# Final output blocks stored from two queues instead of three, and cached keys turned and loaded at other places

## The chip, the core and the metric

The kernel runs on one core of a Trainium2 chip. A core has five engines, each with its own instruction stream, which meet only through semaphores: TensorE (PE in the profile) multiplies matrices into PSUM banks, VectorE (DVE) and ScalarE (ACT) do elementwise work, reductions and the way out of PSUM, GpSimd (POOL) makes masks and issues transfers, and SyncE (SP) only issues transfers. A transfer is issued by one instruction of SP, ACT or POOL and carried out by the core's 16 DMA engines. The metric is the time of one execution on the device in microseconds. Lower is better.

## What is computed

A streaming encoder step with two layers, on 16 meta tokens and 256 new frames of one stream and 32 frames of a running one (304 columns in all, width 2048). All matrices are float32.

```python
for layer in range(DEPTH):                    # DEPTH = 2
    if layer < N_A:                           # layer 0: mLSTM, 8 heads of 512, then the shared K/V
        xp, buf, C, n, m = mlstm_layer(xp, ...)
        xs, buf, C, n, m = mlstm_layer(xs, state_conv[i], state_C[i], state_n[i], state_m[i], ...)
        p_k, p_v, p_logf = shared_kv(xp, kv_norm_g, w_kvf, b_f, k_norm_g)
        s_k, s_v, s_logf = shared_kv(xs, kv_norm_g, w_kvf, b_f, k_norm_g)
        ks_all = concatenate([cache_k, s_k], axis=1)     # 512 cached rows + 32 new ones
        vs_all = concatenate([cache_v, s_v], axis=1)
    else:                                     # layer 1: forgetting attention ("FoX"), 16 heads of 128
        xp = fox_layer(xp, qpos_p, fp[:, N_META:], p_k, p_v, ...)
        xs = fox_layer(xs, qpos_s, fs[:, past:], ks_all, vs_all, ...)

def fox_layer(x, ...):
    q, z = split(rmsnorm(x, norm_g) @ w_in, 2)
    q = rmsnorm(q, q_norm_g)
    o = fox_attend(q, f_q, q_pos, k, v, f_k, k_pos)   # softmax(q k^T + forget terms) v
    return x + (o * silu(z)) @ w_out                  # y_prompt (256 rows) and y_sample (32 rows)
```

The change touches the second layer only: the cached keys and values that the running stream attends to, and the stores of y_prompt and y_sample at the very end.

## The kernel before

The columns are the tokens; the residual stream lies in SBUF turned, as xT (128 partitions, 16 parts of the width, 304 columns). Every weight matrix is streamed through four slots in chunks of 512 rows x 256 columns. For each chunk SP loads it into `raw` (L147), ScalarE makes a rounded copy `w_hi` (L153), VectorE the rest `w_lo` = raw - w_hi (L158), and TensorE does three products for each of eight 128x128 pieces (L178 to L180, 24 matmuls). The semaphore `used` counts the chunks that TensorE has finished, `lo_made` the low parts. ScalarE and VectorE work two chunks ahead of TensorE, and SP may load a slot again once its low part is made.

The attention layer is one list, `order`, of 96 chunks that all engines walk through alike. Q chunks give queries of a group of four heads, Z chunks the gates, OUT chunks multiply with w_out. The list is Q0, then Z0 and Q1, then Z1, Q2 and OUT0, then Z2, Q3 and OUT1, then Z3 and OUT2, and OUT3 at the end, eight chunks each. Each chunk is a slot, to which the tables `QUERIES`, `ATTEND` and `BESIDE` attach events of the attention. In slot n each engine does its part of chunk n (VectorE and ScalarE: the low and high part of chunk n+2), then its part of the slot's events, strictly in that order. The events that matter here, for a group g:

- `q`: TensorE turns the queries to token rows, ScalarE takes them (q_t) and squares them. `r`: VectorE sums the squares (L2567) and scales them (L2570). `n`: ScalarE takes the root (L2463). `f`: VectorE finishes the norms and scales q_t (L210 to L218, L2590, L2593). `s`: VectorE copies two selection matrices (L2583, L2584). `b`: TensorE turns the queries back (L2767), VectorE takes them (qT L2604, q_new L2607).
- `K0` to `K3`: VectorE turns the cached keys Kc of one head into KcT (L2577, `turn_keys`). The first of a group waits until all 16 loads of its keys have landed. Each counts up `blk_made`.
- `X0`, `Y`: TensorE computes the first scores (L2779 to L2781, which need q_new and qT), and the scores with the cached keys (L2793, which need all four KcT).

GpSimd issues the group's loads: 16 for the cached keys (`kc_load`, L2395), the gains (L2401), the new keys (L2405) and three for values (`v_load`, L2408 to L2412). For the first group it does so on its way from the step before; for a later one it waits until the four KcT of the group before are made.

During OUT3 the output is finished: after chunk j VectorE adds the product to xT (L2670), turns two parts of the width into `y_blk` (L2677) and counts up `blk_made`. The function `y_store` then stores the block with 12 transfers: four bands of partitions `a`, each with two parts for y_prompt (L2367, 32 KB each) and one for y_sample (L2371, 8 KB). `Y_PARTS` divides them among three engines, four each: share 0 goes to SP, share 1 to ScalarE (one slot late, behind that slot's high part), share 2 to GpSimd. SP starts on them after its last chunk load. At the end SP waits for the stores of its own and ScalarE's, GpSimd for its own.

Of the kernel before, what the change touches and what calls it, by code (L numbers as in the profile page):

```python
# [44 lines left out]
GROUPS = BH // GRP  # L45
# [55 lines left out]
def settled(own, cell):  # L101

    own.wait()
    own.done(own.eng.tensor_tensor(cell, cell, cell, ALU.mult))  # L105

def trunk(nc, i, o):
    whole = ExitStack()
    with whole:  # L110
        def sem(name):
            return whole.enter_context(nc.semaphore(name))
# [24 lines left out]
        used = sem("used")  # L137
# [1623 lines left out]
        C_FOX = C_OUT + 16 * GROUPS  # L1761
# [47 lines left out]
        def fox_load(sp, n, kind, g, j):  # L1809

            if kind == "OUT":
                load_chunk(sp, n, i["b_w_out"][0, HD * g:HD * (g + 1), CW * j:CW * (j + 1)])
            else:
                col = HD * g + CW * (j // 4) + (D if kind == "Z" else 0)
                load_chunk(sp, n, i["b_w_in"][0, 512 * (j % 4):512 * (j % 4 + 1), col:col + CW])
# [22 lines left out]
        def store_values(eng, g, done):  # L1838
            store(eng, g, "v", v_t, done)
            cols_ = bass.ds(g.times(HD).value, HD)  # L1840
            eng.dma_start(v2_dram[0:256, cols_].rearrange("(t p) c -> p t c", p=P), v_t[:, 0:2, :])\
               .then_inc(done, 16)
            eng.dma_start(v2_dram[256:T, cols_], v_t[0:TAIL, 2, :]).then_inc(done, 16)
# [314 lines left out]
        def kv_tensor(pe):  # L2158
# [87 lines left out]
            def last_values():  # L2246
# [53 lines left out]

        ATTEND = {5: "X0 Y", 6: "E0 EY", 7: "N0 NY X1", 8: "T0 TY E1 z", 9: "OY O0 N1 X2", 10: "T1 E2", 11: "O1 N2 X3",
                  12: "T2 E3", 13: "O2 N3", 14: "T3", 15: "O3"}
        QUERIES = {0: "q", 1: "r n K0 K1", 2: "f K2 K3", 3: "s", 4: "b"}

        BESIDE = {0: {**QUERIES, **ATTEND}, 1: {**QUERIES, **ATTEND, 16: "q", 17: "r", 18: "n", 19: "f", 20: "s", 21: "b"},
                  2: {1: "K0 K1", 2: "K2 K3", **ATTEND, 16: "q", 17: "r", 18: "n", 19: "f", 20: "s", 21: "b"},
# [1 line left out]
        BESIDE[3][7], BESIDE[3][8] = "T0 TY E1", "z OY O0 N1 X2"  # L2308
        PARTS_NEXT = {1: "H0 H1", 2: "H2 H3"}
        PARTS_LAST = {9: "H0", 11: "H1", 13: "H2", 15: "H3"}  # L2310
        Y_PARTS = (((0, (0, 1, 2)), (3, (0,))), ((1, (0, 1, 2)), (3, (1,))), ((2, (0, 1, 2)), (3, (2,))))

        order, at = [], A_FOX

# [34 lines left out]
        def use(g, e, k=0):  # L2349
            return USE[g, e] + k  # L2350

        def freed(eng, u):

            eng.wait_ge(use_free[u % 4], u // 4 + 1)
# [4 lines left out]
        def y_store(eng, j, share, stored):  # L2359

            eng.wait_ge(blk_made, BLK_Y + j + 1)
            for a, parts in Y_PARTS[share]:
                rows_ = slice(32 * a, 32 * a + 32)
                for part in parts:
                    if part < 2:
                        c = P * (2 * j + part) + 32 * a
                        eng.dma_start(o["y_prompt"][0, :, c:c + 32].rearrange("(b i) c -> i b c", i=32),  # L2367
                                      y_blk[rows_, 2 * j + part, 0:SEQ].rearrange("i (b c) -> i b c", c=32))\
                           .then_inc(stored, 16)
                    else:  # L2370
                        eng.dma_start(o["y_sample"][0].rearrange("i (k a j) -> a i k j", a=4, j=32)[a][:, 2 * j:2 * j + 2, :],  # L2371
                                      y_blk[rows_, 2 * j:2 * j + 2, SEQ:TQ]).then_inc(stored, 16)

        def fox_sync(sp):
            for n, kind, g, j, _, _ in order[SLOTS:]:
                fox_load(sp, n, kind, g, j)
                if (kind, g, j) == ("Z", 0, 0):
                    for b in range(3):
                        sp.wait_ge(t_free[b], 3 * GROUPS)
                    store_values(sp, Count(GROUPS - 1), last_out)  # L2380
            for j in range(8):
                y_store(sp, j, 0, y_stored)
            sp.wait_ge(y_stored, 16 * 8 * 8)

        def fox_gpsimd(pool):
            own = Own(pool, pool_own, counted["pool"])

            def heads(g):
                return slice(g * HD, (g + 1) * HD)

            def kc_load(g):
                for x in range(GRP):
                    for a in range(4):
                        src = i["cache_k"][0, :, GRP * g + x, 32 * a:32 * a + 32].rearrange("(b j) d -> j b d", j=32)
                        pool.dma_start(Kc[32 * a:32 * a + 32, x, :].rearrange("j (b d) -> j b d", d=32), src)\  # L2395
                            .then_inc(kc_landed, 16)

            def gq_load(g):
                src = i["q_norm_g"][0].rearrange("h d -> (h d)")[heads(g)]
                for m in range(GRP):  # L2400
                    pool.dma_start(gq[:, m:m + 1], src[m * P:(m + 1) * P].rearrange("(p a) -> p a", a=1))\  # L2401
                        .then_inc(gq_landed, 16)

            def kt_load(g):
                pool.dma_start(kT_in[:, :, :], kT_dram[g]).then_inc(kt_landed, 16)  # L2405

            def v_load(g):
                pool.dma_start(Vc[:, :, :], i["cache_v"][0].rearrange("(t p) h d -> p t (h d)", p=P)[:, :, heads(g)])\  # L2408
                    .then_inc(v_landed, 16)
                pool.dma_start(v_all[:, 0:2, :], v2_dram[0:256, heads(g)].rearrange("(t p) c -> p t c", p=P))\  # L2410
                    .then_inc(v_landed, 16)
                pool.dma_start(v_all[0:TAIL, 2, :], v2_dram[256:T, heads(g)]).then_inc(v_landed, 16)  # L2412

            pool.wait_ge(used, C_FOX)
            settled(own, cell[:, :])
            kc_load(0)
            gq_load(0)
            kt_load(0)
            pool.wait_ge(fox_set, 2)  # L2420
            v_load(0)
            pool.wait_ge(last_out, 80)
            for g in range(1, GROUPS):
                pool.wait_ge(blk_made, BLK_KC + GRP * g)
                settled(own, cell[:, :])
                kc_load(g)
                for t in range(3):
                    freed(pool, use(g - 1, "b", t))
                settled(own, cell[:, :])
                gq_load(g)  # L2430
                pool.wait_ge(use_ready, use(g - 1, "X3") + 1)
                settled(own, cell[:, :])
                kt_load(g)
                pool.wait_ge(use_ready, use(g - 1, "O3") + 1)
                settled(own, cell[:, :])
                v_load(g)
            for j in range(8):
                y_store(pool, j, 2, v_out)
            pool.wait_ge(v_out, 80 * (GROUPS - 1) + 16 * 4 * 8)

        def fox_scalar(act):
            def take_q(g, n, j, tile):
# [93 lines left out]
            for n, kind, g, j, tile, events in order:  # L2536
                if n.a + 2 < C_FOX + len(order):
                    high_part(act, n + 2)
                if (kind, g) == ("OUT", LAST_G) and j:
                    y_store(act, j - 1, 1, y_stored)  # L2540
                if (kind, g) == ("Q", 0):
                    if j == 2:
                        act.wait_ge(fox_set, 2)
                        act.activation(F2[0:BH, :], F_row[:, :], ACT.Copy).then_inc(F_high, 1)
                    if j == 3:
                        counted["values out"](Count(GROUPS - 1))
                    if j == 7:

                        act.wait_ge(k_out, 48 * GROUPS)
                        act.wait_ge(kT_out, 16 * GROUPS)  # L2550
                if kind == "Q" and j in (3, 7):
                    take_q(g, n, j, tile)
                for e in events:
                    event(*e)
# [327 lines left out]
        with nc.Block() as block:  # L2882
            @block.sync
            def _(sp):
                mix_sync(sp)
                kv_sync(sp)
                fox_sync(sp)

            @block.gpsimd
            def _(pool):  # L2890
                mix_gpsimd(pool)
                kv_gpsimd(pool)
                fox_gpsimd(pool)

            @block.scalar
            def _(act):
                mix_scalar(act)
                kv_scalar(act)
                fox_scalar(act)

            @block.vector
            def _(dve):
                mix_vector(dve)
                kv_vector(dve)
                fox_vector(dve)

            @block.tensor
            def _(pe):
                mix_tensor(pe)
                kv_tensor(pe)  # L2910
                fox_tensor(pe)
# [29 lines left out]
```

## Time and profile before

| what | us |
|---|---|
| median of 3 runs | 1647.21 (1646.39 to 1648.58) |
| the profiled execution: its own time | 1647.23 |
| its span, first to last recorded instruction | 1645.4 |
| TensorE busy | 1619.6 (98%) |
| VectorE busy | 1103.6 (67%) |
| ScalarE busy | 770.8 (47%) |
| GpSimd busy | 338.3 (21%) |
| last matmul of the kernel starts | 1635.60 |

The profiled execution is a typical one: its own time is 0.02 us from the median. TensorE is busy almost throughout, so the things to look for are the few places where it is idle and the stretch after its last matmul, in which everything takes place that is not hidden. Busy times of the transfer queues are not in this table: issuing a transfer is recorded (SPq, ACTq and POOL rows), but not counted as busy.

### The profile page before, as it was taken

How to read it: one execution, taken by the hardware profiler on the slowest of the kernel's cores; microseconds unless marked ns; L12 is line 12 of the kernel's file. 1: busy time of each engine (PE TensorE's matmuls, PEld its weight loads, DVE VectorE, ACT ScalarE, POOL GpSimd, SP SyncE). 2: the span in 40 equal slices, each digit the busy share in tenths (PEclk: the TensorE clock that was granted, in tenths of full speed). 3: DMA queues.
4: the chain of work that ended last, by engine and by line, in shares of the span. 5: the costliest groups of instructions: out<-in, count | busy, mean ns of one | idle time of the engine just before them, and what ended most of it. 6: DMA issues, size and time to landing. Idle time of an engine off the chain costs nothing.

```text
span 1645.4 us, 29275 instructions
## 1 busy us (share of the span) xinstructions
PE 1619.6 (98%) x11571; PEld 1551.7 (94%) x11571; DVE 1103.6 (67%) x2117; ACT 770.8 (47%) x1282; POOL 338.3 (21%) x628
## 2 busy tenths in 40 slices
PE   8999999999999999999999999999999999999997
PEld 6999999999989999999999989999999898999997
DVE  5876666766677876868677788656535646563755
ACT  5545344443454443534535445555443454535451
POOL 1210111011234222322323311022105303030004
PEclk9999999999999999999999999999999999999999
DMA  6676667666876666665756655465658756575535
GB/s 193 174 200 165 183 185 207 165 179 182 238 210 225 200 222 195 207 223 175 248 181 206 212 173 171 129 221 181 193 195 243 196 166 147 172 180 164 162 116 109
DMA packets 311480, 308.22 MB, mean 187 GB/s; under 512 B 74408, under 2 KB 290496, under 8 KB 311344
## 3 DMA queue, kind: packets, MB, share of 16 engines
q1 hardware_dynamic: 275472, 224.32, 47.3%
q0 software_dynamic: 28048, 80.36, 15.1%
q10 hardware_dynamic: 7824, 1.68, 0.6%
q8 instruction: 92, 1.51, 0.4%
q14 instruction: 44, 0.36, 0.1%
HBM read 259.49 MB, written 46.79 MB: 186 GB/s over the span
## 4 chain that ended last, share of the span: by engine, by line
PE 89%; DVE 5%; DMA 2%; ACT 2%; issue 1%; SPq 1%; POOL 0%; DVEq 0%; ACTq 0%
PE acc L178 25%; PE acc L180 25%; PE acc L179 24%; PE aux L1515 3%; PE aux L1362 2%; PE aux L1488 2%; DVE w_lo L158 1%; DMA raw<-in_b_w_in 1%; PE aux L1341 1%; PE aux L2781 1%; PE aux L1522 1%; DMA x_tok<-in_x_prompt 1%; PE aux L2169 1%; PE aux L1534 1%; PE aux L2837 0%
## 5 line engine op out<-in xcount | busy, mean ns | idle before, releaser
L158 DVE TENSOR_TENSOR w_lo<-raw,w_hi 128x1024 fp32r<-128x1024 f32 x400 | 485.1, 1219 | 274.4 <-ACT w_hi L153 272.6
L153 ACT ACTIVATE w_hi<-raw 128x1024 fp32r<-128x1024 f32 x400 | 414.8, 1055 | 217.7 <-PE acc L180 191.5
L178 PE MATMUL acc<-xg_hi,w_hi 128*128 128x304 f32 x1536 | 471.1, 307 | 2.2 <-DVE w_lo L158 2.0
L180 PE MATMUL acc<-xg_hi,w_lo 128*128 128x304 f32 x1536 | 464.2, 302 | 0.0
L179 PE MATMUL acc<-xg_lo,w_hi 128*128 128x304 f32 x1536 | 463.1, 301 | 0.0
L178 PEld LDWEIGHTS acc<-xg_hi,w_hi 128*128 128x128 f32 x1536 | 289.6, 189 | 6.3 <-issue 3.6
L105 POOL TENSOR_TENSOR cell<-cell 1x1 f32<-1x1 f32 x151 | 76.1, 504 | 1059.2 <-DVE xc_lo L903 318.8
L179 PEld LDWEIGHTS acc<-xg_lo,w_hi 128*128 128x128 f32 x1536 | 290.4, 189 | 0.8
L180 PEld LDWEIGHTS acc<-xg_hi,w_lo 128*128 128x128 f32 x1536 | 289.8, 189 | 0.0
L178 PE MATMUL acc<-xb_hi,w_hi 128*128 128x288 f32 x512 | 155.9, 305 | 4.5 <-DVE w_lo L158 4.5
L178 PE MATMUL acc<-hz_hi,w_hi 128*128 128x304 f32 x512 | 155.1, 303 | 0.4 <-DVE zs L987 0.4
L180 PE MATMUL acc<-hz_hi,w_lo 128*128 128x304 f32 x512 | 154.8, 302 | 0.0
L179 PE MATMUL acc<-hz_lo,w_hi 128*128 128x304 f32 x512 | 154.7, 302 | 0.0
L180 PE MATMUL acc<-xb_hi,w_lo 128*128 128x288 f32 x512 | 152.2, 297 | 0.0
L179 PE MATMUL acc<-xb_lo,w_hi 128*128 128x288 f32 x512 | 151.9, 297 | 0.0
L178 PEld LDWEIGHTS acc<-xb_hi,w_hi 128*128 128x128 f32 x512 | 96.5, 189 | 6.0 <-DVE w_lo L158 5.6
L178 PEld LDWEIGHTS acc<-hz_hi,w_hi 128*128 128x128 f32 x512 | 96.2, 188 | 1.2 <-DVE hz_lo L1249 0.8
L179 PEld LDWEIGHTS acc<-xb_lo,w_hi 128*128 128x128 f32 x512 | 96.6, 189 | 0.4
L180 PEld LDWEIGHTS acc<-hz_hi,w_lo 128*128 128x128 f32 x512 | 96.7, 189 | 0.0
L179 PEld LDWEIGHTS acc<-hz_lo,w_hi 128*128 128x128 f32 x512 | 96.2, 188 | 0.4
L180 PEld LDWEIGHTS acc<-xb_hi,w_lo 128*128 128x128 f32 x512 | 96.2, 188 | 0.0
L758 ACT ACTIVATE C_out<-aux 128x512 f32<-128x512 f32 x32 | 19.2, 599 | 131.6 <-PE aux L1515 131.6
(489 smaller groups left out, 2944.2 us busy)
## 6 DMA issues: line engine op xcount, KB each, us to landing
raw<-in_a_w_in SPq DMA_DIRECT2D x128, 512.0 KB, 4.0
raw<-in_a_w_out SPq DMA_DIRECT2D x64, 512.0 KB, 4.5
raw<-in_w_kvf SPq DMA_DIRECT2D x64, 512.0 KB, 4.8
raw<-in_b_w_in SPq DMA_DIRECT2D x64, 512.0 KB, 4.8
raw<-in_b_w_out SPq DMA_DIRECT2D x32, 512.0 KB, 3.5
raw<-in_a_wq SPq DMA_DIRECT2D x16, 512.0 KB, 4.2
raw<-in_a_wk SPq DMA_DIRECT2D x16, 512.0 KB, 4.1
raw<-in_a_wv SPq DMA_DIRECT2D x16, 512.0 KB, 5.2
```

What stands on the lines that cost most here:

```text
L105: own.done(own.eng.tensor_tensor(cell, cell, cell, ALU.mult))
L153: act.activation(w_hi[:, s, :, :], raw[:, s, :, :], ACT.Copy).then_inc(hi_made, 1)
L158: dve.tensor_tensor(w_lo[:, s, :, :], raw[:, s, :, :], w_hi[:, s, :, :].bitcast(F32), ALU.subtract).then_inc(lo_made, 1)
L178: pe.matmul(acc[b][:, 0:width], wh, x_hi[:, k0 + k, :], start=st, stop=False)
L179: pe.matmul(acc[b][:, 0:width], wh, x_lo[:, k0 + k, :], start=False, stop=False)
L180: mm = pe.matmul(acc[b][:, 0:width], wl, x_hi[:, k0 + k, :], start=False, stop=last and k == 3)
L758: act.activation(C_out[:, d % 2, :], aux[u.turn(3)][:, :], ACT.Copy).then_inc(b_free[u.turn(3)], 1)
L1341: mm = pe.matmul(gate_sum[r:r + 32, 0:T], wg_in[:, HT * g + d, :], (q_T, k_T, v_T)[g][:, d, :], start=h.a == 0 and g == 0, stop=h.a == LAS ...
L1362: mm = pe.matmul(aux[b][0:n, c:c + T - t0], k_T[:, d, t0:t0 + n], q_T[:, d, t0:T], start=d == 0, stop=d == HT - 1)
L1488: mm = pe.matmul(aux[b][:, :], p_, v_, start=k == 0, stop=t < 2 and k == len(parts) - 1)
L1515: mm = pe.matmul(aux[b][:, :], k_, v_, start=k == 0, stop=k == len(parts) - 1)
L1522: mm = pe.matmul(aux[3][:, :], s_, k_, start=k == 0, stop=k == len(parts) - 1)
```

## The change

Four things are edited.

1. The places of `K0` to `K3` for groups 0 and 1. Before, all four are turned in slots 1 and 2. Now two are turned in slot 0, one in slot 3 behind `s` and one in slot 4 behind `b`. For groups 2 and 3 nothing changes.
2. `kc_load` for group 0 waits between heads until TensorE has used one, two and three chunks of the attention layer.
3. The first `v_load` waits until six chunks of the layer have been used.
4. GpSimd stores no output blocks any more. SP stores eight of the 12 pieces of blocks 0 to 6 and ScalarE four (all for y_prompt); of block 7 each stores six.

```diff
--- before.py
+++ after.py
@@ -2300,7 +2300,7 @@
 
         ATTEND = {5: "X0 Y", 6: "E0 EY", 7: "N0 NY X1", 8: "T0 TY E1 z", 9: "OY O0 N1 X2", 10: "T1 E2", 11: "O1 N2 X3",
                   12: "T2 E3", 13: "O2 N3", 14: "T3", 15: "O3"}
-        QUERIES = {0: "q", 1: "r n K0 K1", 2: "f K2 K3", 3: "s", 4: "b"}
+        QUERIES = {0: "q K0 K1", 1: "r n", 2: "f", 3: "s K2", 4: "b K3"}
 
         BESIDE = {0: {**QUERIES, **ATTEND}, 1: {**QUERIES, **ATTEND, 16: "q", 17: "r", 18: "n", 19: "f", 20: "s", 21: "b"},
                   2: {1: "K0 K1", 2: "K2 K3", **ATTEND, 16: "q", 17: "r", 18: "n", 19: "f", 20: "s", 21: "b"},
@@ -2308,7 +2308,8 @@
         BESIDE[3][7], BESIDE[3][8] = "T0 TY E1", "z OY O0 N1 X2"
         PARTS_NEXT = {1: "H0 H1", 2: "H2 H3"}
         PARTS_LAST = {9: "H0", 11: "H1", 13: "H2", 15: "H3"}
-        Y_PARTS = (((0, (0, 1, 2)), (3, (0,))), ((1, (0, 1, 2)), (3, (1,))), ((2, (0, 1, 2)), (3, (2,))))
+        Y_PARTS = (((0, (0, 1, 2)), (1, (0, 1, 2)), (2, (2,)), (3, (2,))), ((2, (0, 1)), (3, (0, 1))))
+        Y_LAST = (((0, (0, 1, 2)), (1, (0, 1, 2))), ((2, (0, 1, 2)), (3, (0, 1, 2))))
 
         order, at = [], A_FOX
 
@@ -2359,7 +2360,7 @@
         def y_store(eng, j, share, stored):
 
             eng.wait_ge(blk_made, BLK_Y + j + 1)
-            for a, parts in Y_PARTS[share]:
+            for a, parts in (Y_LAST if j == 7 else Y_PARTS)[share]:
                 rows_ = slice(32 * a, 32 * a + 32)
                 for part in parts:
                     if part < 2:
@@ -2380,7 +2381,7 @@
                     store_values(sp, Count(GROUPS - 1), last_out)
             for j in range(8):
                 y_store(sp, j, 0, y_stored)
-            sp.wait_ge(y_stored, 16 * 8 * 8)
+            sp.wait_ge(y_stored, 16 * 12 * 8)
 
         def fox_gpsimd(pool):
             own = Own(pool, pool_own, counted["pool"])
@@ -2388,8 +2389,11 @@
             def heads(g):
                 return slice(g * HD, (g + 1) * HD)
 
-            def kc_load(g):
+            def kc_load(g, since=0):
+
                 for x in range(GRP):
+                    if since and x:
+                        pool.wait_ge(used, since + x)
                     for a in range(4):
                         src = i["cache_k"][0, :, GRP * g + x, 32 * a:32 * a + 32].rearrange("(b j) d -> j b d", j=32)
                         pool.dma_start(Kc[32 * a:32 * a + 32, x, :].rearrange("j (b d) -> j b d", d=32), src)\
@@ -2414,10 +2418,11 @@
 
             pool.wait_ge(used, C_FOX)
             settled(own, cell[:, :])
-            kc_load(0)
+            kc_load(0, C_FOX)
             gq_load(0)
             kt_load(0)
             pool.wait_ge(fox_set, 2)
+            pool.wait_ge(used, C_FOX + 6)
             v_load(0)
             pool.wait_ge(last_out, 80)
             for g in range(1, GROUPS):
@@ -2434,9 +2439,6 @@
                 pool.wait_ge(use_ready, use(g - 1, "O3") + 1)
                 settled(own, cell[:, :])
                 v_load(g)
-            for j in range(8):
-                y_store(pool, j, 2, v_out)
-            pool.wait_ge(v_out, 80 * (GROUPS - 1) + 16 * 4 * 8)
 
         def fox_scalar(act):
             def take_q(g, n, j, tile):
```

On VectorE, the end of Q0 and slots 0 to 2 of group 0. Before (w_lo rows are low parts of chunks, qst the norms of the queries):

```order
L158 TENSOR_TENSOR w_lo<-raw,w_hi 128x1024 x5
L2567 TENSOR_REDUCE qst<-q_sq 128x4 x3
L2570 TENSOR_SCALAR qst<-qst 128x12
L2577 STREAM_TRANSPOSE KcT<-Kc 128x512 x2
L158 TENSOR_TENSOR w_lo<-raw,w_hi 128x1024
```

And now, two lines further down in the file:

```order
L158 TENSOR_TENSOR w_lo<-raw,w_hi 128x1024 x4
L2579 STREAM_TRANSPOSE KcT<-Kc 128x512 x2
L158 TENSOR_TENSOR w_lo<-raw,w_hi 128x1024
L2569 TENSOR_REDUCE qst<-q_sq 128x4 x3
L2572 TENSOR_SCALAR qst<-qst 128x12
L158 TENSOR_TENSOR w_lo<-raw,w_hi 128x1024
```

The first two transposes have moved ahead of one low part and of the sums.

On VectorE, from the last step of `f` in slot 2 to slot 5 of group 0. Before:

```order
L2593 TENSOR_TENSOR q_t<-q_t,qst 128x512 x3
L2577 STREAM_TRANSPOSE KcT<-Kc 128x512 x2
L158 TENSOR_TENSOR w_lo<-raw,w_hi 128x1024
L2656 TENSOR_TENSOR zg<-acc,rstd_row 128x288 x2
L2583 CAST sel_new<-minus 128x128
L2584 CAST sel<-minus 128x512
L158 TENSOR_TENSOR w_lo<-raw,w_hi 128x1024
L2604 TENSOR_TENSOR qT<-aux,gq 128x4x128 x2
L2607 TENSOR_TENSOR q_new<-aux,gq 128x128
L158 TENSOR_TENSOR w_lo<-raw,w_hi 128x1024
```

And now:

```order
L2595 TENSOR_TENSOR q_t<-q_t,qst 128x512 x3
L158 TENSOR_TENSOR w_lo<-raw,w_hi 128x1024
L2658 TENSOR_TENSOR zg<-acc,rstd_row 128x288 x2
L2585 CAST sel_new<-minus 128x128
L2586 CAST sel<-minus 128x512
L2579 STREAM_TRANSPOSE KcT<-Kc 128x512
L158 TENSOR_TENSOR w_lo<-raw,w_hi 128x1024
L2606 TENSOR_TENSOR qT<-aux,gq 128x4x128 x2
L2609 TENSOR_TENSOR q_new<-aux,gq 128x128
L2579 STREAM_TRANSPOSE KcT<-Kc 128x512
L158 TENSOR_TENSOR w_lo<-raw,w_hi 128x1024
```

Two transposes stood between q_t and the low part of slot 3; one of them now stands ahead of q_new and one behind it.

On SP, from the last chunk loads to the first output blocks. Before:

```order
L147 DMA raw<-in_b_w_out 128x4x256 x16
L2367 DMA out_y_prompt<-y_blk 32x8x32 x2
L2371 DMA out_y_sample<-y_blk 32x2x32
L2367 DMA out_y_prompt<-y_blk 32x8x32 x3
L2371 DMA out_y_sample<-y_blk 32x2x32
```

And now:

```order
L147 DMA raw<-in_b_w_out 128x4x256 x16
L2368 DMA out_y_prompt<-y_blk 32x8x32 x2
L2372 DMA out_y_sample<-y_blk 32x2x32
L2368 DMA out_y_prompt<-y_blk 32x8x32 x2
L2372 DMA out_y_sample<-y_blk 32x2x32 x3
L2368 DMA out_y_prompt<-y_blk 32x8x32 x2
L2372 DMA out_y_sample<-y_blk 32x2x32
```

SP's four stores of a block have become eight.

## Rows read from the trace of the kernel before

**Rows 1.** The page, busy time of each engine over the span.

```profile
PE 1619.6 (98%) x11571; PEld 1551.7 (94%) x11571; DVE 1103.6 (67%) x2117; ACT 770.8 (47%) x1282; POOL 338.3 (21%) x628
```

**Rows 2.** Timeline of TensorE, both groups: start, length, instruction [idle before <- releaser].

```profile
1283.49 0.40 PE L178 MATMUL acc<-xb_hi,w_hi 128*128 128x288 f32 x1 [0.66 <-DVE w_lo L158]
...
1287.93 0.40 PE L178 MATMUL acc<-xb_hi,w_hi 128*128 128x288 f32 x1 [0.96 <-DVE w_lo L158]
...
1293.35 0.40 PE L178 MATMUL acc<-xb_hi,w_hi 128*128 128x288 f32 x1 [0.63 <-DVE w_lo L158]
...
1297.28 0.30 PE L2779 MATMUL aux<-F,sel 128*128 128x144 f32 x1 [0.47 <-DVE q_new L2607]
...
1360.40 0.40 PE L178 MATMUL acc<-xb_hi,w_hi 128*128 128x288 f32 x1 [0.84 <-DVE w_lo L158]
...
1366.57 0.40 PE L178 MATMUL acc<-xb_hi,w_hi 128*128 128x288 f32 x1 [1.37 <-DVE w_lo L158]
...
1370.50 0.31 PE L2779 MATMUL aux<-F,sel 128*128 128x144 f32 x1 [0.46 <-DVE q_new L2607]
```

**Rows 3.** Timeline of VectorE, slots 1 to 4 of group 0.

```profile
1282.21 1.22 DVE L158 TENSOR_TENSOR w_lo<-raw,w_hi 128x1024 fp32r<-128x1024 f32 x1 [5.80 <-ACT w_hi L153]
...
1285.34 1.30 DVE L2577 STREAM_TRANSPOSE KcT<-Kc 128x512 f32<-128x512 f32 x2
1286.65 1.22 DVE L158 TENSOR_TENSOR w_lo<-raw,w_hi 128x1024 fp32r<-128x1024 f32 x1
...
1290.89 1.30 DVE L2577 STREAM_TRANSPOSE KcT<-Kc 128x512 f32<-128x512 f32 x2
1292.11 1.18 DVE L158 TENSOR_TENSOR w_lo<-raw,w_hi 128x1024 fp32r<-128x1024 f32 x1
...
1296.74 0.29 DVE L2607 TENSOR_TENSOR q_new<-aux,gq 128x128 f32<-128x128 f32 x1
```

**Rows 4.** Timeline of ScalarE, high parts in slots 1 and 2 of group 0.

```profile
1281.12 1.06 ACT L153 ACTIVATE w_hi<-raw 128x1024 fp32r<-128x1024 f32 x1 [1.68 <-DMA raw<-in_b_w_in]
...
1285.58 3.88 ACT L153 ACTIVATE w_hi<-raw 128x1024 fp32r<-128x1024 f32 x4
```

**Rows 5.** Timeline of ScalarE: it takes queries once TensorE has used the fourth Q0 chunk.

```profile
1259.23 0.71 ACT L2448 ACTIVATE qf<-acc 128x288 f32<-128x288 f32 x2 [1.95 <-PE acc L180]
```

**Rows 6.** Timeline of GpSimd, loads of the first group.

```profile
1253.84 10.29 POOL L2395 DMA_DIRECT2D Kc<-in_cache_k  x16
...
1266.83 0.77 POOL L2408 DMA_DIRECT2D Vc<-in_cache_v  x1
```

**Rows 7.** Timeline of SP's queue during OUT3, stores of output blocks.

```profile
1616.64 0.52 SPq L2367 DMA_DIRECT2D out_y_prompt<-y_blk  x1
...
1620.35 0.45 SPq L2367 DMA_DIRECT2D out_y_prompt<-y_blk  x1
...
1631.98 1.34 SPq L2371 DMA_DIRECT2D out_y_sample<-y_blk  x1
...
1634.33 0.32 SPq L2367 DMA_DIRECT2D out_y_prompt<-y_blk  x1
...
1637.53 0.32 SPq L2367 DMA_DIRECT2D out_y_prompt<-y_blk  x1
1637.88 0.45 SPq L2367 DMA_DIRECT2D out_y_prompt<-y_blk  x1
1638.38 0.46 SPq L2371 DMA_DIRECT2D out_y_sample<-y_blk  x1
1638.88 0.43 SPq L2367 DMA_DIRECT2D out_y_prompt<-y_blk  x1
```

**Rows 8.** The chain that ended last, its last piece.

```profile
1639.41 1.06 POOL out_y_sample L2371 x2
```

**Rows 9.** DMA issues from 1605 us on: KB each, median us from issue to landing.

```profile
out_y_sample<-y_blk POOLq DMA_DIRECT2D x16, 8.0 KB, 2.5
...
out_y_sample<-y_blk SPq DMA_DIRECT2D x8, 8.0 KB, 2.2
```

## The prediction

> **What bounds the kernel now.** I read the page's busy times first: TensorE works through 98% of the span [rows 1], so an edit elsewhere counts only if it closes one of TensorE's gaps, or lies behind the last matmul. Next TensorE's timeline of the attention layer. The reader is to see seven gaps there, three before low parts and one before the first scores in group 0, two and one in group 1 [rows 2]: 0.66 + 0.96 + 0.63 + 0.47 + 0.84 + 1.37 + 0.46 = 5.39 us. This is all that the new places of K0 to K3 and the pacing could win. Last the end of the chain of waits and the queues in OUT3. The chain runs out in GpSimd's issues: its last one ends at 1639.41 + 1.06 = 1640.47 [rows 8], and the span of 1645.4 ends 4.9 us later. In that time the last transfer lands (2.5 us from the start of its issue, so 2.0 from its end [rows 9]), and 2.9 us are left for waits and closing. SP had issued its last store at 1638.88 + 0.43 = 1639.31 [rows 7]. So SP was 1.2 us ahead of the end, with four stores per block.
>
> **K0 and K1 into slot 0.** Before, they fill 1285.34 to 1286.64, and the low part follows at 1286.65 [rows 3]. It looks as if they hold it up. But that low part also needs its high part, the first of four that take 3.88 us from 1285.58 [rows 4]: 0.97 each, done at 1286.55, with a short pass between engines. The high part waits for nothing of K0 and K1: it stands behind the root of the norms, which needs the sums that VectorE finishes before them. So ScalarE gives the same moment, and I cost this at 0. The gap of 0.96 stays; so does the 0.66 ahead of it, which comes from a chunk that lands late (ScalarE waits for it until 1281.12 [rows 4]). In slot 0 the transposes cost nothing, as VectorE is idle for 5.80 us ahead of 1282.21 [rows 3]; they need the keys landed, which were issued by 1264.13 [rows 6]. Group 1 has the same order, with its gap of 0.84, and I take 0 there too. The bounds of this term are 0 and, if the high part came earlier for another reason, a gain of the whole gap, 0.96 and 0.84.
>
> **K2 and K3 into slots 3 and 4.** Here the high part is ready (the second of the four ends near 1287.5), and the low part of slot 3 waits for VectorE alone. K2 and K3 move it from 1290.89 to 1292.11, 1.22 us [rows 3]. Without them the gaps of 0.63 and 1.37 close, the second but for 1.37 - 1.22 = 0.15. Then the next thing is late: q_new. VectorE must pass K2 (0.61, half of 1.22) before it, so q_new comes only 1.22 - 0.61 = 0.61 us earlier, and TensorE meets it with a longer wait than the 0.47 and 0.46 of before [rows 2]. What closes before the low part beyond 0.61 opens again before the scores. The sum is 0.61 in each group, 1.2 us together. K3 is done 0.61 us after q_new, beside the first scores, whose own products take longer than that before the cached keys are wanted (q_new to scores with KcT: 1296.74 + 0.29 to more than a microsecond behind 1297.28). GpSimd waits for K3 before it loads the next group's keys, some 4 to 5 us later than now; they are wanted in the next group, whose first scores come 73 us after these [rows 2]. Bounds of the two terms together: 0, if something else in the slot is as late, and 0.61 to 1.37 each, so at most 2.0 us.
>
> **The paced loads.** Each of these waits is over before GpSimd reaches it. Its 16 key loads run from 1253.84, 0.64 us each, so it comes to the second, third and fourth head at 1256.4, 1259.0 and 1261.6 [rows 6]. TensorE has finished its fourth chunk at 1259.2 [rows 5] and takes 3.2 us for one (the period of SP's blocks, 1634.33 to 1637.53 [rows 7]); so its first, second and third are done by about 1249.6, 1252.8 and 1256.0. The sixth is done at 1259.2 + 6.4 = 1265.6, the values are issued at 1266.83 [rows 6]. The term is 0; if the last wait did bind, it would be by a microsecond, and TensorE is 16 us from the first gap.
>
> **The stores.** TensorE gives a block every 3.2 us, and SP now has eight stores for each. What does SP need for one? Where it waits for a block, the first takes 0.35 to the next start, the others 0.50 (1637.53, 1637.88, 1638.38, 1638.88). Where it is behind, seven go out from 1616.64 to 1620.35, 0.53 each [rows 7]. Eight at 0.50 are 4.0 us against 3.2: SP falls behind by 0.8 us or more with each block and never waits for one again. Its end is then a plain sum. It has 7 x 8 + 6 = 62 stores. It starts them behind its last chunk load, at 1616.64 before, and that start moves with TensorE, to 1615.4. 62 x 0.50 = 31.0, so its last issue ends at 1646.4. The even split of block 7 comes too late to help. From the end of the last issue to the end of the span I take 4.7: landing takes 2.2 us from the start of the issue for SP against 2.5 for GpSimd [rows 9], less 0.46 for the issue, so 1.74, and the same 2.9 behind it. The span ends at 1651.1, 5.7 us later than before. ScalarE's six for block 7 would be out by 1636.3 + 3.0 = 1639.3, and hide beside SP. GpSimd's 32 stores are gone from the path, which is worth nothing, as SP is late by more. At 0.47 a store (small ones weigh more in SP's new mix, so I think this low) SP's last issue ends at 1644.5 and the span at 1649.2; at 0.53 it is 1648.3 and 1653.0. A single store of 1.34 us [rows 7], 0.88 over the usual, could come again.
>
> The Trainium skill weighs against this term. "DMA: Bandwidth & Descriptors", section "Issuing engines are not separate DMA queues", says that several issuing engines only save the sequencer's time for starting a transfer, which is usually small beside the transfer itself. Here that time is the resource: 0.50 us for each of 62 small transfers, which in themselves overlap. By the rule's "usually small" the sum would be the gain of 1.2 us alone, the second rival below.
>
> **Sum.** Gain 0 + 1.2 + 0 in the attention, then an end 5.7 us later (the gain is already in SP's start). 1645.4 + 5.7 = 1651.1 of span, with 1.8 us around it (1647.23 against 1645.4), 1652.9. The profiled execution is 0.02 us from the median, so no correction is due.
>
> **Rivals.** First, SP falls behind, but less, and the gaps close further: 0.47 a store and 2.0 us instead of 1.2 gives 1649.2 - 0.8 + 1.8 = 1650.2. That is still slower and belongs to my forecast's range, 1650.2 to 1656.5 (0.53 a store, no gain at all and one long store: 1653.0 + 1.2 + 0.9 + 1.8 = 1656.9, cut a little since all three must meet).
>
> Second, SP keeps pace. This needs a store at 0.40 or less. For it speaks the 0.35 after a wait, and that the profiler's own records may make an issue longer than it is in the timed runs. Against it, seven at 0.53 in a row. Block 7 would be ready at 1637.5 - 1.2 = 1636.3, six stores at up to 0.50 end at 1639.3, and with 4.7 the span ends at 1644.0: 1645.8 in time, 1.4 less than before. It decides below 0.40; between 0.40 and 0.46 the time lies between 1645.8 and 1650.4, mostly no measurable change.
>
> Third, the pacing binds after all and lets the chunk before 1281.12 land in time. Then the gaps behind it could close as well, all 5.39 us. With SP's end as forecast the time is 1652.9 - 4.2 = 1648.7, within no change; only together with the second rival would it be faster, 1641.6. The waits that are over before they are reached speak against it.
>
> Fourth, the keys are not there in slot 0. VectorE would stand still with all its low parts behind K0. The last keys are issued at 1264.1 and K0 comes when the low part of slot 0 is done, at least 5.80 us before 1282.21, so about 1276.4: a margin of 12 us, of which a landing would have to take all. If it took 2 us more, TensorE would lose about 2, 1654.9.
>
> **Chances.** Forecast with its own range 0.77; second rival and the stretch up to 0.46 0.12; third 0.05, a tenth of it with the second; fourth and other stalls 0.06. A measurement of this kernel tells about 0.2%, 3.3 us, from no change. Slower by more than that (over 1650.5): almost all of the forecast's case and the fourth, 0.81. Within: 0.15. Faster (under 1643.9): 0.04. The range takes in the third rival's time and the upper end: 1648.6 to 1656.5.
>
> **What would show it.** In the profile after, SP's stores stand one behind the other without a wait from the first to the last, 0.50 apart, and its last issue ends near 1646, 7 us behind ScalarE's; the chain ends in SP. TensorE's last matmul starts 1.2 us earlier, near 1634.4. The gaps of 0.66, 0.96 and 0.84 are still there, those of 0.63 and 1.37 are gone, and the two before the first scores have grown. GpSimd's first loads stand where they stood. I am wrong in the main if SP waits for blocks 4 to 7, and wrong in the small terms if TensorE ends more than 2 us earlier or no earlier.

## The result and the profile after

| | before | after |
|---|---|---|
| median, 20 runs each, us | 1647.37 | 1650.71 |
| lowest to highest | 1644.87 to 1649.62 | 1648.54 to 1653.67 |
| span of the profiled execution | 1645.4 | 1648.0 |
| output block 7 ready | 1637.5 | 1635.9 |
| SP's last issue ends | 1639.3 | 1646.5 |
| from block 7 ready to the end of the span | 7.9 | 12.0 |

(The last row is taken from the unrounded times of the two traces, as all such differences below.)

The ratio is 1.0022, interval 1.0015 to 1.0028: slower by 2.5 to 4.6 us. The prediction was 1652.9, slower by 5.7. Way and range were right, the size was too large by some 2 us. The profiled execution of the changed kernel took 1649.77, which is 0.9 below its median, so the profiles differ by 2.5 us where the medians differ by 3.3.

The timeline of TensorE after the change, against [rows 2] (start, length, instruction, idle before <- releaser):

```profile
1283.28 0.40 PE L178 MATMUL acc<-xb_hi,w_hi 128*128 128x288 f32 x1 [0.88 <-DVE w_lo L158]
...
1287.73 0.40 PE L178 MATMUL acc<-xb_hi,w_hi 128*128 128x288 f32 x1 [0.97 <-DVE w_lo L158]
1296.48 0.31 PE L2781 MATMUL aux<-F,sel 128*128 128x144 f32 x1 [0.77 <-DVE q_new L2609]
...
1359.68 0.41 PE L178 MATMUL acc<-xb_hi,w_hi 128*128 128x288 f32 x1 [0.84 <-DVE w_lo L158]
...
1364.65 0.40 PE L178 MATMUL acc<-xb_hi,w_hi 128*128 128x288 f32 x1 [0.19 <-DVE w_lo L158]
...
1369.17 0.30 PE L2781 MATMUL aux<-F,sel 128*128 128x144 f32 x1 [1.06 <-DVE q_new L2609]
```

The gap of 0.63 is gone, that of 1.37 is down to 0.19, and the two before the first scores have grown from 0.47 and 0.46 to 0.77 and 1.06. To get the gain free of where the execution stood before, take the stretch from the first to the last row of a group: 1283.49 to 1297.28 was 13.79, now 13.20; 1360.40 to 1370.50 was 10.10, now 9.49. So 0.59 and 0.61. (In group 0 the idle times shown add up to only 0.33 less, 0.96 + 0.63 + 0.47 against 0.97 + 0.77. The other 0.26 came with the gap of 0.63 going altogether. In group 1, where 0.19 of the gap is left, the idle times are 0.57 less for the 0.61. So closing a gap gave back more than the idle time that the view had for it.)

The timeline of VectorE after, slots 0 to 2 of group 0, against [rows 3]:

```profile
1276.51 1.30 DVE L2579 STREAM_TRANSPOSE KcT<-Kc 128x512 f32<-128x512 f32 x2
1282.00 1.23 DVE L158 TENSOR_TENSOR w_lo<-raw,w_hi 128x1024 fp32r<-128x1024 f32 x1 [4.19 <-ACT w_hi L153]
...
1286.45 1.23 DVE L158 TENSOR_TENSOR w_lo<-raw,w_hi 128x1024 fp32r<-128x1024 f32 x1 [1.23 <-ACT w_hi L153]
```

The two transposes lie in the idle time of slot 0. Where they were, VectorE is now idle for 1.23 us and waits for ScalarE's high part, as forecast: the transposes had stood in that wait and had not made it.

SP's queue after: its first store, one in the middle and its last two.

```profile
1615.09 0.50 SPq L2368 DMA_DIRECT2D out_y_prompt<-y_blk  x1
...
1638.89 0.32 SPq L2372 DMA_DIRECT2D out_y_sample<-y_blk  x1
...
1645.57 0.45 SPq L2368 DMA_DIRECT2D out_y_prompt<-y_blk  x1
1646.07 0.45 SPq L2372 DMA_DIRECT2D out_y_sample<-y_blk  x1
```

62 stores in 1646.52 - 1615.09 = 31.4 us, 0.507 each, against 31.0 forecast. They stand back to back but for one pause of 0.34 us, behind the 46th store and ahead of the row at 1638.89. It is no wait for a block: that store still belongs to block 5. ScalarE's last issue ended at 1638.8.

What did not come out is the time behind. The span ends 1.4 us after SP's last issue, not 4.7. First the moment from which the end is counted, block 7 ready (the end of its transpose), before and after:

```profile
1636.67 0.83 DVE L2677 STREAM_TRANSPOSE y_blk<-xT 128x288 f32<-128x288 f32 x2
```

```profile
1635.11 0.83 DVE L2679 STREAM_TRANSPOSE y_blk<-xT 128x288 f32<-128x288 f32 x2
```

```profile
L2882 POOLq EVENT_SEMAPHORE  x2: 17/17/17, 1645.2 to 1645.3; - x2
...
L2882 ACTq DRAIN  x1: 150/150/150, 1639.4 to 1639.4; - x1
...
L2882 SPq DRAIN  x1: 7/7/7, 1641.5 to 1641.5; - x1
L2882 POOLq COMPARE_BRANCH  x1: 38/38/38, 1641.7 to 1641.7; - x1
L2882 POOLq DRAIN  x1: 3335/3335/3335, 1641.9 to 1641.9; - x1
L2882 SPq EVENT_SEMAPHORE  x1: 17/17/17, 1645.4 to 1645.4; - x1
```

After:

```profile
L2884 POOLq EVENT_SEMAPHORE  x2: 17/17/17, 1647.8 to 1647.9; - x2
...
L2884 POOLq DRAIN  x1: 10697/10697/10697, 1513.0 to 1513.0; - x1
...
L2884 ACTq DRAIN  x1: 150/150/150, 1638.9 to 1638.9; - x1
...
L2884 SPq DRAIN  x1: 7/7/7, 1647.7 to 1647.7; - x1
```

Before, everything had landed by 1641.7, and then GpSimd alone drained for 3.3 us: the kernel was waiting for nothing that moves data. After, GpSimd stores nothing; its drain begins behind its last loads at 1513 and is over by 1523.7, so it is hidden entirely. SP's drain takes 7 ns.

### The profile page after: what moved, and what is told of

The parts are those of the page before. It is cut to its first block, busy times and chain, and to the rows that moved or that the text cites. A ratio compares the mean times of both kernels' runs of the same rounds, so it can differ in the third digit from the quotient of the medians.

```text
span 1648.0 us, 29275 instructions
## 1 busy us (share of the span) xinstructions
PE 1618.8 (98%) x11571; PEld 1551.0 (94%) x11571; DVE 1103.6 (67%) x2117; ACT 770.8 (47%) x1282; POOL 318.6 (19%) x596
## 4 chain that ended last, share of the span: by engine, by line
PE 89%; DVE 4%; DMA 2%; ACT 2%; issue 1%; SPq 0%; POOL 0%; ACTq 0%; DVEq 0%
PE acc L178 25%; PE acc L180 25%; PE acc L179 24%; PE aux L1515 3%; PE aux L1362 2%; PE aux L1488 2%; DVE w_lo L158 1%; DMA raw<-in_b_w_in 1%; PE aux L1341 1%; PE aux L2783 1%; DMA x_tok<-in_x_prompt 1%; PE aux L1522 1%; PE aux L2169 1%; PE aux L1534 1%; ACT w_hi L153 0%
```

## The experiments

All ratios are to the kernel before. "Tail" is the time in the profiled execution from block 7 ready (its transpose's end) to the end of the span; it is free of what TensorE did earlier and so much finer than the timed ratios: the three kernels with the stores of before agree in it within 0.1 us, the two with GpSimd up to block 5 as well, the two with 62 stores on SP within 0.3. From "GpSimd stores up to block 6" on, every kernel also has the new places of the keys and none has the pacing, so its ratio has the gain of the keys in it and its tail has not. Each "tail" and "span" is of one execution.

| kernel | ratio, interval | span | tail |
|---|---|---|---|
| before | 1 | 1645.4 | 7.9 |
| the changed kernel | 1.0022, 1.0015 to 1.0028 | 1648.0 | 12.0 |
| new places of the keys alone | 0.9994, 0.9985 to 1.0003 | 1643.9 | 7.8 |
| new stores alone | 1.0028, 1.0017 to 1.0039 | 1651.5 | 12.3 |
| pacing alone | 1.0002, 0.9993 to 1.0011 | 1646.0 | 7.9 |
| SP 7 and ScalarE 5 stores of 12 | 0.9989, 0.9980 to 0.9999 | 1644.4 | 8.3 |
| GpSimd stores up to block 6 | 0.9984, 0.9975 to 0.9993 | 1642.2 | 6.0 |
| the same, one store of block 7 too | 0.9991, 0.9982 to 1.0000 | 1644.2 | 7.3 |
| the same as up to block 6, GpSimd waits for all | 1.0001, 0.9992 to 1.0010 | 1644.7 | 9.3 |
| GpSimd stores up to block 5 | 0.9970, 0.9958 to 0.9981 | 1641.9 | 4.6 |
| the same, all keys in slot 0 | 0.9969, 0.9957 to 0.9981 | 1640.0 | 4.6 |

### The parts alone

The places of the keys alone:

```diff
-        QUERIES = {0: "q", 1: "r n K0 K1", 2: "f K2 K3", 3: "s", 4: "b"}
+        QUERIES = {0: "q K0 K1", 1: "r n", 2: "f", 3: "s K2", 4: "b K3"}
```

> The kernel before with the new places of K0 to K3 alone. Theory (the changed kernel's gaps): q_new comes 0.61 us earlier in each of groups 0 and 1, TensorE ends 1.2 us earlier, the end behind it is as before: span 1644.2, ratio 0.9993. Rival (the 1.56 us by which TensorE ends earlier in the changed kernel come from the pacing as well, or from chance): 0 to 0.5 us. If GpSimd's part of the end were all that matters, nothing changes in it here.

The time is not told apart from before (0.9994), but the gaps are those of the changed kernel:

```profile
1283.50 0.40 PE L178 MATMUL acc<-xb_hi,w_hi 128*128 128x288 f32 x1 [1.06 <-DVE w_lo L158]
...
1296.70 0.30 PE L2779 MATMUL aux<-F,sel 128*128 128x144 f32 x1 [0.77 <-DVE q_new L2607]
...
1359.89 0.40 PE L178 MATMUL acc<-xb_hi,w_hi 128*128 128x288 f32 x1 [0.84 <-DVE w_lo L158]
...
1369.38 0.30 PE L2779 MATMUL aux<-F,sel 128*128 128x144 f32 x1 [1.07 <-DVE q_new L2607]
```

13.20 and 9.49 us: 0.59 and 0.61 less than before, the same as with the whole change. Its tail is that of before, its drain again 3335 ns.

The stores alone:

```diff
-        QUERIES = {0: "q K0 K1", 1: "r n", 2: "f", 3: "s K2", 4: "b K3"}
+        QUERIES = {0: "q", 1: "r n K0 K1", 2: "f K2 K3", 3: "s", 4: "b"}
-            kc_load(0, C_FOX)
+            kc_load(0)
-            pool.wait_ge(used, C_FOX + 6)
```

(against the changed kernel)

> The changed kernel with the old places of K0 to K3 and without the pacing, so the new stores alone. Theory (62 stores of 0.50 us on SP are a plain sum that starts with SP's last chunk load): the last issue ends at 1616.6 + 31.3 = 1647.9, the span 1.5 later, 1649.4, 4.0 us above before, ratio 1.0024. Rival (part of the loss of the changed kernel is TensorE's or the DMA engines'): another sum, and SP's stores not back to back.

1.0028, and 62 stores from 1618.31 to 1650.06, 0.512 each. The span of 1651.5 is 2.1 above the expected 1649.4. Of this 1.7 is a later start: in this execution block 7 was ready at 1639.2, 1.7 later than in that of the kernel before, for reasons that lie ahead of the stores. 0.45 is the stores' own, 31.75 us in place of 31.3. The tail, 12.3, has neither the start nor the keys in it and is that of the changed kernel, 12.0. So the stores are the whole loss. The keys give back 1.2 of it by the gaps; the timed ratios, 1.0028 and 1.0022, agree with that but can't show it by themselves.

The pacing alone (the three lines of `kc_load` and the wait before `v_load`, put into the kernel before):

```diff
+            def kc_load(g, since=0):
+
                 for x in range(GRP):
+                    if since and x:
+                        pool.wait_ge(used, since + x)
...
+            kc_load(0, C_FOX)
...
+            pool.wait_ge(used, C_FOX + 6)
             v_load(0)
```

> The kernel before with the paced first loads alone. Theory: each wait is over when GpSimd comes to it, so its first loads start where they did, within 0.1 us, and the time is the same, ratio 1.000. Rival (pacing makes chunks land in time or late): the gap of 0.66 us and its followers change, up to 2 us either way.

No change: 1.0002, and GpSimd's first loads, against [rows 6], are where they were, with the same 10.29 us for 16:

```profile
1253.93 10.29 POOL L2398 DMA_DIRECT2D Kc<-in_cache_k  x16
...
1266.92 0.77 POOL L2411 DMA_DIRECT2D Vc<-in_cache_v  x1
```

### The number of stores on SP

```diff
-        Y_PARTS = (((0, (0, 1, 2)), (1, (0, 1, 2)), (2, (2,)), (3, (2,))), ((2, (0, 1)), (3, (0, 1))))
-        Y_LAST = (((0, (0, 1, 2)), (1, (0, 1, 2))), ((2, (0, 1, 2)), (3, (0, 1, 2))))
+        Y_PARTS = (((0, (0, 1, 2)), (1, (0, 1, 2)), (2, (2,))), ((2, (0, 1)), (3, (0, 1, 2))))
+        Y_LAST = (((0, (0, 1, 2)), (1, (0,))), ((1, (1, 2)), (2, (0, 1, 2)), (3, (0, 1, 2))))
```

(against the changed kernel)

> The changed kernel (two queues, GpSimd stores nothing, its closing drain long over) with SP's 62 stores cut to 7 x 7 + 4 = 53 and ScalarE's raised to 7 x 5 + 8 = 43. Theory (a store costs its queue 0.49 us, SP's are a plain sum from 1615.1): 9 stores fewer are 4.4 us less; SP's last issue ends at 1615.1 + 26.0 = 1641.1, the span 1.5 later, 1642.6, against 1648.0 of the changed kernel, ratio to before 0.998. ScalarE's last block starts at 1636 and takes 8 x 0.49, 1639.9, so it hides. Rival (not the count on SP but two queues as such, or the transfers themselves, make the end late): the span stays within 1 us of 1648.0.

53 stores from 1615.33 to 1642.83, 27.5 us, 1.5 more than expected. One of them took 1.73 us, 1.3 over the usual, and there is again a pause of 0.33 behind the 46th. The span is 3.6 us below that of the changed kernel for nine stores fewer, where 5.4 were expected, and ends 1.6 us after the last issue. (By the timed ratios, 0.9989 against 1.0022, it is 5 us.) So the count on SP sets the end; two queues as such do not.

### GpSimd's drain

Four kernels leave GpSimd's share as it was for the first blocks and end it earlier or later. All have the new places of the keys. The first gives GpSimd blocks 0 to 6 (edit against the kernel with the new places alone):

```diff
+        Y_LAST = (((0, (0, 1, 2)), (1, (0, 1, 2))), ((2, (0, 1, 2)), (3, (0, 1, 2))), ())
...
-            for a, parts in Y_PARTS[share]:
+            for a, parts in (Y_LAST if j == 7 else Y_PARTS)[share]:
...
-            sp.wait_ge(y_stored, 16 * 8 * 8)
+            sp.wait_ge(y_stored, 16 * (8 * 7 + 12))
...
-            for j in range(8):
+            for j in range(7):
                 y_store(pool, j, 2, v_out)
-            pool.wait_ge(v_out, 80 * (GROUPS - 1) + 16 * 4 * 8)
+            pool.wait_ge(v_out, 80 * (GROUPS - 1) + 16 * 4 * 7)
```

> New places of the keys, no pacing; blocks 0 to 6 stored by three queues with four stores each as before, block 7 by SP and ScalarE with six each. Theory A (a kernel whose last store is GpSimd's ends 4.9 us after that issue, one whose last is SP's 1.5 us; GpSimd pays some 3 us at its end): block 7 is ready at 1636.3, six stores end at 1639.3, span 1640.8; GpSimd's last store ends at 1635.7, and 4.9 later is 1640.6, hidden. 4.6 us below before, ratio 0.9972. Theory B (the 4.9 us are not GpSimd's, the short end of the changed kernel comes from the lull in the queues while SP works alone): about 4.7 after the last issue, span 1644.0, ratio 0.9991.

Neither theory's number fits: 1642.2 lies between 1640.8 and 1644.0. Its closing instructions show the reason:

```profile
L2883 POOLq EVENT_SEMAPHORE  x2: 17/17/17, 1642.0 to 1642.1; - x2
...
L2883 POOLq DRAIN  x1: 4642/4642/4642, 1637.3 to 1637.3; - x1
...
L2883 SPq DRAIN  x1: 7/7/7, 1640.5 to 1640.5; - x1
```

The drain starts at 1637.3, as soon as GpSimd's own stores have landed, but it lasts 4.6 us now and ends at 1641.9; SP is there at 1640.5. GpSimd still holds the end, by 1.4 us. So theory A has the right cause, a price at GpSimd's end, but took it for smaller than it is here. The next two kernels move the drain. With one small store of block 7 left to GpSimd (against the kernel up to block 6):

```diff
-        Y_LAST = (((0, (0, 1, 2)), (1, (0, 1, 2))), ((2, (0, 1, 2)), (3, (0, 1, 2))), ())
+        Y_LAST = (((0, (0, 1, 2)), (1, (0, 1, 2))), ((2, (0, 1, 2)), (3, (0, 1))), ((3, (2,)),))
-            sp.wait_ge(y_stored, 16 * (8 * 7 + 12))
+            sp.wait_ge(y_stored, 16 * (8 * 7 + 11))
```

(and GpSimd's loop and count again to block 7)

> As the kernel with GpSimd up to block 6, but GpSimd also stores one small piece of block 7, ScalarE five. Theory C (GpSimd's closing drain, 3.3 us in the kernel before and 4.6 us with GpSimd up to block 6, follows its last landing and holds the end): its store is issued at 1636.4 to 1637.0 and lands at 1638.4, the drain ends at 1641.8 (3.3) to 1643.1 (4.6), span 1642.0 to 1643.3. Rival (the drain is an artefact, the end comes from SP and ScalarE): five and six stores end at 1639.0, span 1640.5.

The drain starts at 1639.2, takes 4.72 us, and the span ends at 1644.2, 0.9 above the upper figure of theory C: the drain began 0.7 later than assumed, 0.5 of it because block 7 was ready only at 1636.8, and it took 0.1 more. From block 7 ready it is 7.3 us, within 0.6 of the kernel before, for a single store of 8 KB. With GpSimd waiting at the end for stores that are not its own (against the kernel up to block 6):

```diff
             pool.wait_ge(v_out, 80 * (GROUPS - 1) + 16 * 4 * 7)
+            pool.wait_ge(y_stored, 16 * (8 * 7 + 12))
```

> As the kernel with GpSimd up to block 6, but GpSimd waits at its end until the stores of SP and ScalarE have landed too, at about 1640.4, though it issues none of them. Theory C1 (the drain is a fixed price of GpSimd's end once it has issued stores, however long ago): it starts at 1640.4 and lasts 3.3 to 4.6 us, span 1643.9 to 1645.2. Theory C2 (the drain waits for something that runs on after GpSimd's own last transfers and is over by itself): it is short here, 0 to 1.7 us, span 1640.8 to 1642.2.

```profile
L2884 SPq DRAIN  x1: 7/7/7, 1639.8 to 1639.8; - x1
...
L2884 POOLq DRAIN  x1: 4642/4642/4642, 1639.9 to 1639.9; - x1
```

The same 4642 ns to the nanosecond, though it starts 5.2 us after its last issue ends (1.8 in the kernel up to block 6), and 3.6 us after the last landing of its own, at 1636.3 (0.2 in the kernel up to block 6). This is theory C1. So it is not a wait for transfers in flight: it is something of the same length that begins when GpSimd reaches its end. The span ends 4.9 us behind SP's readiness, and the gain of the kernel is gone (1.0001).

Last, GpSimd stores blocks 0 to 5 only, which leaves its drain room (against the kernel up to block 6):

```diff
-            for a, parts in (Y_LAST if j == 7 else Y_PARTS)[share]:
+            for a, parts in (Y_LAST if j > 5 else Y_PARTS)[share]:
...
-            sp.wait_ge(y_stored, 16 * (8 * 7 + 12))
+            sp.wait_ge(y_stored, 16 * (8 * 6 + 12 * 2))
-            for j in range(7):
+            for j in range(6):
...
-            pool.wait_ge(v_out, 80 * (GROUPS - 1) + 16 * 4 * 7)
+            pool.wait_ge(v_out, 80 * (GROUPS - 1) + 16 * 4 * 6)
```

> Three queues for blocks 0 to 5, SP and ScalarE with six each for blocks 6 and 7. Theory C: GpSimd's last store is issued by 1632.4 and landed by 1633.8, so a drain of up to 4.6 us is over by 1638.4 and hidden; SP and ScalarE have six stores of 0.48 in 3.2 us for block 6 and keep pace; their last issue ends at 1639.0, lands at 1640.4, span 1640.8, 1.4 us below the kernel with GpSimd up to block 6 and 4.6 below before, ratio 0.9972. Rival (the 1.6 us between landing and end there are not GpSimd's): span 1642.2 again.

```profile
L2883 POOLq DRAIN  x1: 4315/4315/4315, 1635.3 to 1635.3; - x1
...
L2883 ACTq DRAIN  x1: 150/150/150, 1640.2 to 1640.2; - x1
...
L2883 SPq DRAIN  x1: 7/7/7, 1641.7 to 1641.7; - x1
```

The drain is over at 1639.6 and hidden; SP closes. The tail is 4.6 us, 3.3 below before, and the ratio 0.9970: 3 to 7 us faster, the best of the stores. Some of the ratio is the keys' (0.9994 alone); the tail is the stores' alone. Its span of 1641.9 is 1.1 above the expected 1640.8 because block 7 was ready 1.1 us later than in the kernel up to block 6; the profiled execution is the slowest of its six, 1643.77 against a median of 1641.62.

### All keys in slot 0

```diff
-        QUERIES = {0: "q K0 K1", 1: "r n", 2: "f", 3: "s K2", 4: "b K3"}
+        QUERIES = {0: "q K0 K1 K2 K3", 1: "r n", 2: "f", 3: "s", 4: "b"}
```

(against the kernel up to block 5)

> The same stores, and all four K0 to K3 of groups 0 and 1 in slot 0. Theory (K2 in front of q_new gives back 0.61 of the 1.22 us that the low part gains): q_new now comes 1.22 us earlier than before in both groups, TensorE ends 0.6 to 0.8 us earlier than with two in slot 0, span 1640.1, ratio 0.9968. VectorE is idle 5.8 and 6.9 us in slot 0 and the four take 2.5. Rival (something else in slots 3 and 4 is as late): no gain, span 1640.8.

```profile
1283.43 0.40 PE L178 MATMUL acc<-xb_hi,w_hi 128*128 128x288 f32 x1 [0.95 <-DVE w_lo L158]
...
1296.41 0.30 PE L2780 MATMUL aux<-F,sel 128*128 128x144 f32 x1 [0.40 <-DVE q_new L2608]
...
1359.76 0.40 PE L178 MATMUL acc<-xb_hi,w_hi 128*128 128x288 f32 x1 [1.01 <-DVE w_lo L158]
...
1368.66 0.30 PE L2780 MATMUL aux<-F,sel 128*128 128x144 f32 x1 [0.47 <-DVE q_new L2608]
```

The waits for q_new are back at 0.40 and 0.47, and the stretches are 12.98 and 8.90, so 0.22 and 0.59 less than with K2 in slot 3. The gap at 1288.0, inside the first stretch, has grown by 0.15, which the 0.22 already has in it. The gap at 1359.8, ahead of the second, has grown by 0.17, which comes off: 0.6 us is left, the lower end of the 0.6 to 0.8 expected. The timed runs can't tell that: 0.9969 against 0.9970. One of its six executions took 4075.91 us, for which I have no cause; the other five, of which the ratio is made, lie between 1640.66 and 1642.31. It has the shortest span of all, 1640.0, but in time it is no more than equal to the kernel up to block 5.

## Why the prediction was right, and what was off

**The keys.** Right as worked out. K0 and K1 gave nothing, since the high part came at the same moment. K2 and K3 gave 0.59 and 0.61, forecast 0.61 each: the low part gains 1.22, K2 gives half of it back before q_new. All keys in slot 0 confirms the second half of the argument. The sum was 1.2. TensorE's block 7 came 1.6 us earlier: 0.2 of this was there before the first gap (1283.28 against 1283.49), and 0.2 came behind the scores of group 1, which started 1.33 earlier (1369.17 against 1370.50). No run shows that the change has a hand in either.

**The paced loads.** Right: 0, and the run with the pacing alone shows it.

**SP's sum.** Right. 62 stores, 0.507 each, 31.4 us against 31.0. The even split of block 7 came too late, ScalarE's six hid. But 0.507 is not the price of a plain store: one issue was held for 1.17 us, 0.7 over the usual, like the long store of [rows 7] that I kept for the upper end, and one pause took 0.34. Without the two it is 0.49 each. I took 0.50 from a stretch that had neither, so a hundredth too much on each store paid for most of what I had left out.

**The end behind the last issue.** This is the term that was mis-sized. I took 4.9 us behind GpSimd's last issue, took off a landing of 2.0, and carried the remaining 2.9 over to SP as "waits and closing", as if it belonged to the end of the program. Of this 2.9 nearly all was GpSimd's drain of 3.3, which began a little before my estimate of the landing. With GpSimd out, SP's last store landed 1.5 us from the start of its issue, so 1.0 from its end in place of 1.74, and closing took 0.4 in place of 2.9: 1.4 in all in place of 4.7, 3.3 less. SP's last issue ended 0.1 later than forecast, and the two together are the 1651.1 forecast against the span of 1648.0. So the sentence that failed is that taking GpSimd off the stores "is worth nothing, as SP is late by more": it was worth its drain, 3.3 us. It was bought with 31 us of issues on SP. The kernel up to block 5 has the one without the other.

**The range.** That the time lies in the forecast's own range, 1650.2 to 1656.5, owes something to luck. The range had bounds for a store, for the gaps and for one long issue, and none for this term, which was off by 3.3 us. With 1.4 in it the sum would have been 1649.6, below that range. The profiled execution took 1649.77; the median of 20 is 1650.71.

**The rule weighed.** The Trainium skill, "DMA: Bandwidth & Descriptors", section "Issuing engines are not separate DMA queues", calls the sequencer's time for starting a transfer usually small beside the transfer. For one store the trace agrees in the main: SP's issues took a median of 0.45 us, and its stores of 32 KB and 8 KB landed 1.8 and 1.6 us from the start of the issue. But the landings overlap and the issues do not, so for 62 in a row on one queue, 0.507 us each, the issues set the end. The sum of 1645.8 that the rule would give was not met.

**The rivals.** SP did not keep pace (0.507, where it needed 0.40). The pacing did not bind. The keys were there in slot 0: K0 ran at 1276.51, right behind a low part.

## What to carry to other kernels

At the end of a kernel, count stores per queue and multiply by the issue time of a back-to-back stretch (0.50 us here). Where that exceeds the time between blocks, the queue is a sum of its own, and the compute engines set only its start. Read the closing instructions too before a time is carried from one engine to another: the end behind GpSimd's last transfer is not the end behind SP's. Where three queues are needed, let GpSimd stop first and give the last blocks to the other two. By an estimate from these runs its last issue has to end some 5 us before theirs: at 3.5 us its drain still held the end by 1.4, at 6.7 it was hidden.

## What the runs showed of the hardware

GpSimd's closing drain goes by how many output stores it had issued, not by when it starts: 4315 ns for 24 (in two kernels), 4642 for 28 (at two starts, 2.6 us apart), 4723 for 29, so 82 ns a store. The 29th is a store of 8 KB, the four between 24 and 28 are of both sizes, so it is the count and not the bytes. This rests on three counts. With 32 it is only 3335, in three kernels, which is what the same line gives for 12 stores (4315 - 12 x 81.75 = 3334, with 81.75 the step per store from 24 to 28). There the timeline shows a pause between GpSimd's first two stores of block 7, behind its 29th, which no other block has:

```profile
1638.83 0.58 POOL L2367 DMA_DIRECT2D out_y_prompt<-y_blk  x1 [0.44 <-issue]
```

It could be that part of the work is done there, but no run tests that, and a pause alone doesn't show it: SP pauses for 0.33 to 0.34 us behind its 46th store in all three kernels where it has so many, and ScalarE for 0.31 to 0.33 behind its seventh in all eleven. With no stores the drain takes 10.7 to 10.9 us from right behind large loads, part of which may be their landing.

SP and ScalarE were held at the same time once in each of the eleven profiled executions, beginning between 1629.4 and 1633.2: before, SP's store at 1631.98 took 1.34 us and ScalarE's at 1632.04 took 1.29. In the changed kernel SP's at 1630.05 took 1.17 and ScalarE's at 1629.97 took 1.27. In each of them one 16 KB packet of the queue that the profile calls "instruction" begins within 0.4 us of it and lasts 0.9 to 1.4 us; the kernel before, from 1631.9 to 1632.9:

```profile
q8 instruction: 1, 0.02, 6.0%
```

So a load of instructions may be what holds both queues. That the two coincide is shown, that one causes the other is not.
